# Scores of the first attention in three one-pass products of rounded halves, for its third to eighth pair of heads

## The reference, cut to what matters

```python
s_c = jnp.einsum('bqghd,bngd->bghqn', qb, k_cmp) * scale
s_s = jnp.einsum('bqghd,bgqkd->bghqk', qb, k_sel) * scale
s_w = jnp.einsum('bqghd,bkgd->bghqk', qb, kwb) * scale
...
o = gb[..., 0:1] * o_c + gb[..., 1:2] * o_s + gb[..., 2:3] * o_w
...
merged = g_a * (y_pool @ w_proj_pool[l]) + g_b * (y_nsa @ w_proj_nsa[l])
x = x + merged @ w_out[l]
```

## Time and profile before

| | us |
|---|---|
| median of 3 runs | 1510.26 (1510.06 to 1510.4) |
| the profiled execution | 1510.39 |
| its span, first to last instruction | 1508.5 |
| granted TensorE clock, mean | 0.998 of full speed |
| PE busy | 1492.9 (99%) |
| DVE, ACT, POOL busy | 898.6, 774.7, 739.0 |

### The profile page before, as it was taken

How to read it: one execution, slowest core, us unless ns; L and a number is a source line. 1 busy time by engine, 2 the same in 40 slices (tenths; PEclk the granted TensorE clock), 3 DMA queues, 4 the chain that set the end, 5 groups by cost and what they waited for, 6 DMA issues and landing times.

```text
span 1508.5 us, 19815 instructions
## 1 busy us (share of the span) xinstructions
PE 1492.9 (99%) x7411; PEld 1183.4 (78%) x7411; DVE 898.6 (60%) x1447; ACT 774.7 (51%) x1237; POOL 739.0 (49%) x462
## 2 busy tenths in 40 slices
PE   9999999999999999999999999999999999999997
PEld 7776677788888888888887777777888888888885
DVE  5567776534336764847546523532102699999998
ACT  5575676533344223241344634632224688888885
POOL 3465566644785646565464654743547262141100
PEclk9999999999999999999999999999999999999999
DMA  9210010133243554654221431122226299999984
GB/s 374 76 66 24 20 43 29 65 112 139 99 154 126 198 205 158 230 191 177 89 100 71 123 116 43 68 73 70 98 98 263 103 357 411 404 394 383 392 333 179
DMA packets 74943, 250.87 MB, mean 166 GB/s; under 512 B 11713, under 2 KB 13057, under 8 KB 74841
## 3 DMA queue, kind: packets, MB, share of 16 engines
q1 hardware_dynamic: 67264, 234.41, 41.6%
q0 software_dynamic: 4752, 8.19, 1.5%
q10 hardware_dynamic: 2824, 6.94, 1.3%
HBM read 244.94 MB, written 12.66 MB: 171 GB/s over the span
## 4 chain that ended last, share of the span: by engine, by line
PE 95%; DVE 3%; ACT 1%; issue 1%; DMA 0%; DVEq 0%; ACTq 0%
PE ps L463 18%; PE ps L467 18%; PE ps L464 18%; PE ps L1128 4%; PE ps L1132 4%; PE ps L1129 4%; PE ps L703 2%; PE ps L729 2%; PE ps L691 2%; PE ps L524 2%; PE ps L1161 2%; PE ps L527 2%; PE ps L1157 2%; PE ps L530 2%; PE ps L1158 2%; PE ps L560 2%
## 5 line engine op out<-in xcount | busy, mean ns | idle before, releaser
L321 POOL TENSOR_TENSOR RS<-RAW,RS 128x1024 fp32r<-128x1024 f32 x172 | 429.8, 2502 | 350.1 <-ACT RS L312 346.5
L312 ACT ACTIVATE RS<-RAW 128x1024 fp32r<-128x1024 f32 x305 | 320.1, 1056 | 226.1 <-PE ps L467 133.1
L463 PE MATMUL ps<-RH,RS 128*128 128x512 f32 x784 | 309.3, 394 | 0.2 <-DVE TB L1977 0.2
L467 PE MATMUL ps<-RH,RS 128*128 128x512 f32 x784 | 305.4, 390 | 0.0
L464 PE MATMUL ps<-RH,RS 128*128 128x512 f32 x784 | 305.2, 389 | 0.0
L463 PEld LDWEIGHTS ps<-RH,RS 128*128 128x128 f32 x784 | 147.2, 188 | 34.3 <-issue 4.8
L467 PEld LDWEIGHTS ps<-RH,RS 128*128 128x128 f32 x784 | 147.2, 188 | 31.1
L464 PEld LDWEIGHTS ps<-RH,RS 128*128 128x128 f32 x784 | 147.3, 188 | 29.8 <-issue 0.2
L321 DVE TENSOR_TENSOR RS<-RAW,RS 128x1024 fp32r<-128x1024 f32 x132 | 155.9, 1225 | 5.9 <-ACT RS L312 5.7
L463 PE MATMUL ps<-RA,RS 128*128 128x512 f32 x400 | 157.7, 394 | 0.0
L464 PE MATMUL ps<-RA,RS 128*128 128x512 f32 x400 | 155.7, 389 | 0.0
(11 more groups left out here) (453 smaller groups left out, 2706.9 us busy)
## 6 DMA issues: line engine op xcount, KB each, us to landing
RAW<-in_w_ff SPq DMA_DIRECT2D x64, 512.0 KB
RAW<-in_w_gate SPq DMA_DIRECT2D x45, 512.0 KB, 18.3
RAW<-in_w_up SPq DMA_DIRECT2D x43, 512.0 KB, 16.2
RAW<-in_w_down SPq DMA_DIRECT2D x42, 512.0 KB, 15.5
PB<-in_ada SPq DMA_DIRECT2D x24, 512.0 KB, 3.7
TB<-in_ada SPq DMA_DIRECT2D x24, 512.0 KB, 3.7
RAW<-in_w_gb SPq DMA_DIRECT2D x16, 512.0 KB
RAW<-in_w_ga SPq DMA_DIRECT2D x16, 512.0 KB
```

Source lines behind the costliest of these rows:

```text
L312: act.activation(RS[:, spl[n], 0, :], raws[slot[n]], ACT.Copy).then_inc(*HI.up(n))
L321: eng.tensor_tensor(RS[:, s, 1, :], raws[slot[n]], hif(RS[:, s, 0, :]), ALU.subtract).then_inc(*mark.up(n))
L463: pe.matmul(b[:, :], wh, xh, start=(k == 0), stop=False)
L467: last = pe.matmul(b[:, :], wl, xh, start=False, stop=(k == K - 1))
```

## The change

The scores of s >= 4 (pairs 2 to 7) are made from halves, like the dense tiles: query high x key high, query low x key high, query high x key low, three one-pass matmuls for each block and head in place of one float32 matmul, and the two heads alternate within a term. For this

- ACT copies the four key blocks to the rounded type (`kh`, two each in steps 2 and 3, into `TMP` 1 to 3 and `TAB` 1), and DVE subtracts in steps 4 and 5 (`kl`, in place in `M`).
- For pair p = 2 to 7 ACT copies the queries to `RA[:, 0, p, :]` in step 2p-1 (`qh`), and DVE subtracts at the start of step 2p into `RA[:, 1, p, :]` (`ql`). These places get the outputs of pair p later.
- PE waits for `ql` before the first scores of a pair, for `kl` before s = 4 and 5.
- Gate results, the mask of the compressed branch (`MCB`) and its sums (`SCS`) move to other places; two gates wait for `ql`. ACT's load of `xT` moves from ahead of m = 4 to m = 7 and waits for `mgsum` 0 in place of `mga` 7.

```diff
-    MCB = RAW2[:, 2, 0:128]
+    MCB = M[:, 6, 256:384]
+    KH = [TMPR[:, 1, :], TMPR[:, 2, :], TMPR[:, 3, :], TABR[:, 1, :]]
...
-    SCS = [RAW2[:, 2, 128:160], RAW2[:, 2, 160:192]]
-    GATE = {("w_gb", m): X[:, m - 1, :] if m else TMP[:, 0, :] for m in range(8)}
-    for m, place in enumerate((TMP[:, 1, :], TMP[:, 2, :], TMP[:, 3, :], TAB[:, 0, :], TAB[:, 1, :], VV[:, 0, :], VV[:, 1, :],
+    SCS = [M[:, 6, 384:416], M[:, 6, 416:448]]
+    GATE = {("w_gb", m): TMP[:, 0, :] if m == 0 else X[:, m - 1 if m < 3 else m, :] for m in range(8)}
+    for m, place in enumerate((X[:, 2, :], TAB[:, 0, :], TMP[:, 1, :], TMP[:, 2, :], TAB[:, 1, :], VV[:, 0, :], VV[:, 1, :],
...
         def nsa_scores(s):
-                pe.wait_ge(*V(("q", pr)))
+                pe.wait_ge(*V(("q", pr) if pr < 2 else ("ql", pr)))
             if s < 2:
                 pe.wait_ge(*A(("k", 8 + br)))
+            elif 4 <= s < 6:
+                pe.wait_ge(*V(("kl", br)))
             for i in (3, 2, 0, 1):
...
-                for a in range(2):
-                    b = ps["ns", s, a, x] if o else take(("ns", s, a, x), ring(s))
-                    h = slice(64 * a, 64 * a + 64)
-                    pe.matmul(b[:, o:o + w], X[h, pr, 128 * i:128 * i + 128], Kd[h, br, (pr // 4 + a) % 2, 0:w], start=True,
-                              stop=True).then_inc(*P.up(("nsc", s, a, i)))
+                bs = [ps["ns", s, a, x] if o else take(("ns", s, a, x), ring(s)) for a in range(2)]
+                for term in range(1 if s < 4 else 3):
+                    for a, b in enumerate(bs):
+                        h, kb = slice(64 * a, 64 * a + 64), 2 * br + (pr // 4 + a) % 2
+                        if s < 4:
+                            q, k = X[:, pr, :], M[:, kb, :]
+                        else:
+                            q, k = RA[:, 1 if term == 1 else 0, pr, :], MR[:, kb, :] if term == 2 else KH[kb]
+                        last = pe.matmul(b[:, o:o + w], q[h, 128 * i:128 * i + 128], k[h, 0:w], start=(term == 0),
+                                         stop=(s < 4 or term == 2))
+                        if s < 4 or term == 2:
+                            last.then_inc(*P.up(("nsc", s, a, i)))
...
+            if n in (2, 3):
+                for kb in range(2 * n - 4, 2 * n - 2):
+                    act.wait_ge(*V(("q", 7)))
+                    act.activation(KH[kb], M[:, kb, :], ACT.Copy).then_inc(*A.up(("kh", kb)))
+            if 3 <= n < 14 and n % 2 == 1:
+                p = (n + 1) // 2
+                if p == 7:
+                    act.wait_ge(*P(("cb", 3)))
+                act.activation(RA[:, 0, p, :], X[:, p, :], ACT.Copy).then_inc(*A.up(("qh", p)))
             if n in LATE:
                 hi_half(act, LATE[n])
...
-        act.wait_ge(*V(("mga", 7)))
-        for i in range(4):
-            act.dma_start(X[:, 2 * i:2 * i + 2, :], t["xT"][:, 2 * i:2 * i + 2, :]).then_inc(*XL[i].up(1))
...
         for m in range(4, 8):
+            if m == 7:
+                act.wait_ge(*G(("mgsum", 0)))
+                for i in range(4):
+                    act.dma_start(X[:, 2 * i:2 * i + 2, :], t["xT"][:, 2 * i:2 * i + 2, :]).then_inc(*XL[i].up(1))
...
+            elif (name, m) == ("w_ga", 0):
+                after(("ql", 2))
+            elif name == "w_gb" and m > 2:
+                after(("ql", m))
...
         for n in range(18):
+            if n in (4, 5):
+                for kb in range(2 * n - 8, 2 * n - 6):
+                    dve.wait_ge(*A(("kh", kb)))
+                    dve.wait_ge(*P(("nsc", n - 2, 1, 1)))
+                    tt(MR[:, kb, :], M[:, kb, :], hif(KH[kb]), ALU.subtract, ("kl", n - 4))
+            if 4 <= n < 16 and n % 2 == 0:
+                dve.wait_ge(*A(("qh", n // 2)))
+                tt(RA[:, 1, n // 2, :], X[:, n // 2, :], hif(RA[:, 0, n // 2, :]), ALU.subtract, ("ql", n // 2))
             if n > 1 and n in STEP_GATE:
                 scaled_gate(*STEP_GATE[n])
```

More of the change, by code:

```diff
@@ L177, in build_program @@
     X = sb("X", [128, 8, S])
+    with nc.sbuf_tensor("MR", [128, 8, S], F32R) as MR:
+        pass
     M = sb("M", [128, 8, S])
@@ L183, in build_program @@
     PC = sb("PC", [128, 4, S])
+    with nc.sbuf_tensor("TABR", [128, 2, S], F32R) as TABR:
+        pass
     TAB = sb("TAB", [128, 2, S])
     VV = sb("VV", [128, 2, S])
+    with nc.sbuf_tensor("TMPR", [128, 4, S], F32R) as TMPR:
+        pass
     TMP = sb("TMP", [128, 4, S])
```

## The result

The changed kernel took 1513.72 us (median of 22 executions, 1510.82 to 1516.3), the kernel before 1510.44 us (22 executions, 1510.06 to 1512.58). The ratio is 1.0018 with a 95% interval of [1.0012, 1.0023], so it is slower by 1.8 to 3.5 us, around the bound of 0.2%. The forecast was 1511.1 us in a range of 1507.9 to 1514.2. In what follows, "the clock falls" means that TensorE's granted clock goes from 2.4 to 1.2 GHz for a stretch.

What follows compares the result with a forecast made beforehand. PE, holding 95% of the chain that ended last, was taken to bound the kernel. Stalls of 3.3 + 0.4 + 0.2 less 3.0 gained gave +0.9 us on the profiled 1510.39, a median of 1511.1 us, range 1507.9 to 1514.2.

Steps and rivals of the forecast that it cites:

- Gain per score step: PE, twelve changed score steps: three one-pass products beat fp32 by 0.25 us each, 3.0 us together, bounds 1.2 to 4.8.
- rival (b): Score products: a one-pass pair costs just half an fp32 pair, gain 0.37 us a step, 1509.8 us; chance 0.12.
- rival (d): Score products: one-pass matmuls on the two row halves don't overlap, 1533 us with the stalls; chance 0.14 including half ways.
- Scores(3): ACT's kh0 and kh1 copies delay DVE's PCR subtraction, so PE's pause in scores(3) grows by 1.04 us.
- Scores(4): POOL's tensor_tensor gets between DVE's key subtractions; scores(4) starts 3.3 us later, 1.04 from scores(3), about 2.25 new idle.
- rival (a): Before scores(4), POOL does not collide with kl: loss 1.1 us instead of 3.3, 1509.0 us; chance 0.17.
- Scores(10) and the small waits: PE waits 0.4 us for ql 5 before scores(10); bank waits in steps without a dense tile cost 0.2 us together.
- The load of xT: ACT's load of xT moved from m=4 to m=7 costs nothing; without its cover, one landing, 7 us.
- The sum: Whole kernel: 3.3 + 0.4 + 0.2 - 3.0 = +0.9 us, a median of 1511.1 us.
- the last rival: TensorE's clock falls to 1.2 GHz in the new idle: 3 us lost, 1514 us; chance 0.04.

Runs made afterwards that it cites:

- run 1: Changed kernel, with GpSimd waiting for ql 2 before the low half of the weight tile that step 3 splits late: 1510.42 us, ratio 0.9996.
- run 5: On top of run 1, scores of the third to eighth pair as one fp32 product of the high halves, low terms left out: 1513.02 us, ratio 1.0008.
- run 4: Changed kernel, with ScalarE's copies kh0 and kh1 moved to the end of its step 2: 1511.44 us, ratio 1.0002.
- run 6: Kernel before, with only the later load of xT from the change: 1511.95 us, ratio 1.0001.
- run 2: Changed kernel, with nine 512-column products of ready data on TensorE ahead of its wait at scores(4): 1511.32 us, ratio 1.0006.
- run 3: On top of run 1, scores(4) also waits for GpSimd's weight half, which it doesn't need: 1514.55 us, ratio 1.0023.
- run 12: Changed kernel, with three 512-column products ahead of TensorE's wait for the fourth norm's root: 1513.15 us, ratio 1.0016.
- run 11: Kernel of run 8, with three 512-column products ahead of TensorE's wait for the fourth norm's root: 1512.76 us, ratio 1.0016.
- run 8: Kernel before, with one extra 1024-column GpSimd operation that scores(4) waits for, old products kept: 1514.50 us, ratio 1.0022.
- run 7: The rearranged version: run 1 plus ScalarE's kh and qh copies moved, and GpSimd making the low halves of kh0 and kh1: 1507.92 us, ratio 0.9979.
- run 10: Kernel of run 7, with three 512-column products ahead of TensorE's wait for the fourth norm's root: 1507.61 us, ratio 0.9978.
- run 9: Kernel before, with three 512-column products ahead of TensorE's wait for the fourth norm's root: 1510.39 us, ratio 0.9997.

## Why the prediction was right in its sum and wrong in its clock

**Gain per score step.** Forecast 0.25 us, twelve times 3.0. Measured: in run 1 the nine steps from scores(4) to scores(15) with no other wait around them gain 2.13 together, 0.22 to 0.26 each, so the products alone gave some 2.8, and the term was 0.2 too large. Run 5 against run 1, 2.1 to 2.5 for all, has the small waits in it that are counted below (0.3 and 0.1), and agrees. The pair starts of scores(9) in the changed kernel show the parts:

```profile
210.75 0.49 PE L705 MATMUL ps<-TMPR,RA 64*128 64x512 f32 x1
211.09 0.39 PE L705 MATMUL ps<-TABR,RA 64*128 64x512 f32 x1
211.09 0.39 PE L705 MATMUL ps<-TMPR,RA 64*128 64x512 f32 x1
211.31 0.40 PE L705 MATMUL ps<-MR,RA 64*128 64x512 f32 x2
211.55 0.34 PE L705 MATMUL ps<-TABR,RA 64*128 64x384 f32 x1
...
211.73 0.34 PE L705 MATMUL ps<-TABR,RA 64*128 64x384 f32 x1
...
211.90 0.34 PE L705 MATMUL ps<-MR,RA 64*128 64x384 f32 x2
212.09 0.22 PE L705 MATMUL ps<-TABR,RA 64*128 64x128 f32 x1
```

At 512 columns the starts are 0.34 (with the switch), 0.22 and 0.24 us apart, at 384 0.18, 0.17 and 0.19. The 0.227 and 0.174 taken from the dense tile's row were right, and rival (b), half of an fp32 pair, is out. It was also what follows from the formula that the Trainium skill ("TensorE: Matmul & The Clock Gate", "Back-to-back issue gap") gives for an isolated matmul, 0.216 and 0.163; by it a gain of 0.37 a step is estimated, and the measured one is 0.24. One-pass products on the two halves of the rows do overlap (both start at 211.09), so rival (d) is out as well.

**Scores(3).** Forecast 1.04 us late. PE resumed at 137.96, 0.86 after the 137.10 of the earlier trace rows; scores(3) itself had begun 0.28 earlier in this profile, so the delay is 1.1. The pause grew by more, from 0.29 to 2.07, since the new loop takes the banks of both heads before the first head's product and so meets the wait one product earlier (PE stops at 135.89 instead of 136.81, 0.28 of it the offset). That costs little time, since the two heads' products then run side by side, but it makes the idle 0.64 us longer: run 4, where PE resumes as early as before, keeps a pause of 1.02 us instead of 0.29. The prediction did not see this, and a longer idle may matter for the clock.

**Scores(4).** Forecast 3.3 us in all, 2.25 of them new idle. Measured 3.15 (3.43 from scores(3)) and 2.23. Run 1 took 2.06 of it away (2.17). This step was right in mechanism and size, rival (a) being what run 1 made.

**Scores(10) and the small waits.** Forecast 0.4 and 0.2. The step into scores(10) has 0.06 us more than before instead of 0.24 less, so 0.3. Another 0.1 goes between scores(7) and scores(8). In the rearranged version, where qh5 comes a step earlier and PE does not pause at scores(10), 0.18 of the 0.24 are still missing there. And from the last dense matmul to the first product of scores(10) it is 0.42 us in the changed kernel, 0.32 before, so that the wait itself is 0.1 and not 0.4. So ql 5 is only a part; what holds the rest was not found.

**The load of xT** costs nothing (run 6).

**The sum** was +0.9 us against the profile of before, 1511.1 us. The lowest three executions of the changed kernel, at a mean clock of 0.998 as before, are those at 1510.82 to 1511.16, and with the pause filled (run 2) the lower group is at 1510.98 to 1511.32. From scores(3) to the last matmul the profile of run 2, in which the clock does not fall, is 0.8 us longer than that of before (1363.95 against 1363.13). The sum was right to 0.2 us.

**The step that failed** is the last rival's chance. It was stated that the clock could fall in the new idle, priced near 1514 us, and given 0.04. In 17 of 22 executions the time is 1512.6 us or more and the mean clock lower, and that took the median there: 3.28 us over the kernel before, of which some 0.6 are the sum above and 2.7 the clock. Runs 2 and 3 show it from both sides: hardly any idle and no fall there, with everything else kept; the idle without the collision, and the fall again. So it is luck that the median lies inside the stated range, 0.5 us from its upper end: that end was made of a larger stall and a smaller gain than those that came, and 6 of the 22 executions lie above it. Two things were overlooked. The idle at scores(4) was set against the end of the kernel, where PE stops for good, and not against short pauses. And it was treated as one pause, where there are two, 14 us apart, with transposes and 64-row products between them.

**What stays open.** Behind the pause at scores(4) the clock was low for 6.8 us in all four profiles of kernels that have both the pause and the three-term products (the changed kernel, runs 3, 4 and 12). In the kernel before with the same pause and the norm's filled (run 11) the times allow one step of 1.6 us and no more; in run 8 the three executions at 1516 us can be that step and the norm's, or a longer one. Whether the products, the earlier pause in scores(3), or the up to 0.5 us by which the pause is longer makes the difference was not told apart. Nor can a single run say in which executions the clock falls; only how often.

## What to carry to other kernels

Price a new stall on TensorE twice: once as its length, and once as the clock that it may cost, here 1.5 to 1.6 us for 3.4 us at half speed, and 3.2 us for 6.8 (scores(4) to scores(5) took 16.15 us in the changed kernel and 12.93 in run 1). Look for a second pause near it as well, though whether the two act together is not shown here. If a stall can't be removed, a few products of data that lie ready, into a bank that is overwritten anyway, can keep the clock: it gave some 2.4 us here, and scores(4) started no later for it (3.45 us late from scores(3), against 3.43). And when an engine gets a short chain of SBUF subtractions on the path, order behind it the other engine's subtraction that would hold it up: one wait on GpSimd was worth 2.1 us. With that wait, ScalarE's copies moved behind what PE waits for (1.0 us) and the other moves of run 7, the change became a gain of 2.8 us (run 10 against run 9, medians).

## What the runs showed of the hardware

- A pause of 0.66 us behind one-column products can be enough to let TensorE's clock fall: the profiles of runs 1, 6, 7 and 8 show it there for about 3.4 us. The length of a pause alone doesn't decide it: near 126 us all 14 profiles have one of 0.8 to 0.9 us, and near 190 us one of 0.66 to 0.74, and in none did the clock fall there. The fall at the norm explains the two groups of times, 1510.4 and 1512 us, that the kernel before has in every session (32 of 98 executions in the upper one). Three matmuls of 512 columns remove the upper one (11 of 11 executions within 0.5 us).
- The fall can come in a pause or behind it. In run 1 the clock fell 0.2 us before PE resumed at the norm, in run 12 0.2 us before it resumed in scores(3); in run 5 it fell 0.4 us after, and at scores(4) in the changed kernel 1.1 us after.
- A GpSimd tensor_tensor that becomes ready while VectorE is in one of several back-to-back subtractions goes between them: the pair of subtractions took 2.17 us longer, and the second ended 0.5 us after GpSimd's 2.53 us were over. It does not wait for VectorE's queue to run dry.
- Two subtractions of 512 columns took GpSimd 2.52 us and VectorE 1.29. While GpSimd made them in run 7 (139.2 to 141.8), VectorE's mask operations, which read one input from PSUM and one from SBUF, took as long as in the kernel before (0.42 us at 256 columns), but a product of four columns with both inputs in SBUF took 0.78 us instead of 0.17 and ended with GpSimd's second subtraction. VectorE's rows, first in the kernel before, then in run 7:

```profile
139.56 0.42 DVE L1961 CUSTOM_DVE_ANT_0 TB<-ps,M 128x256 f32<-128x256 f32 x1
...
140.87 0.17 DVE L1762 TENSOR_TENSOR stat<-stat,RT 128x4 f32<-128x4 f32 x1
```
```profile
139.69 0.42 DVE L1994 CUSTOM_DVE_ANT_0 TB<-ps,M 128x256 f32<-128x256 f32 x1
...
141.00 0.78 DVE L1795 TENSOR_TENSOR stat<-stat,RT 128x4 f32<-128x4 f32 x1
```

The Trainium skill ("SBUF — State Buffer", section "SBUF: two separate sides") says that a GpSimd operation and a VectorE operation with two SBUF inputs hold the shared ports one at a time, each for its whole instruction. The key subtraction held up in the changed kernel, the product held up here and the free mask operations agree with it.
